# The opening of a hybrid encoder step: token tiles turned in threes, two projections chunk by chunk

## What is computed

```python
def rmsnorm(x, g):
    xf = x.astype(jnp.float32)
    y = xf * lax.rsqrt(jnp.mean(xf * xf, axis=-1, keepdims=True) + EPS) * g.astype(jnp.float32)
    return y.astype(x.dtype)

def even_layer(x, ...):
    h = rmsnorm(x, g_pre)
    proj = jnp.einsum('bld,de->ble', h, w_in)
    u, v, za, zb, xbc, dt_raw = jnp.split(proj, EVEN_SPLITS, axis=-1)
    ya, v_rows = gmlp_branch(u, v, za, ws, bs, gv)
    yb, s_fin, new_ctx = ssd_branch(zb, xbc, dt_raw, ...)
    ...

def ssd_branch(zb, xbc, dt_raw, ...):
    xbc, new_ctx = causal_dwconv(xbc, conv_ctx, conv_w, conv_b)
    xbc = jax.nn.silu(xbc)
    ...
    dt = jax.nn.softplus(dt_raw + dt_bias)
    a = -jnp.exp(a_log)
    # in the recurrence: acs = cumsum(dt * a), exp(acs) and so on
```

## Time and profile before

| what | value |
|---|---|
| median of three runs | 1696.01 us |
| the profiled execution | 1696.7 us, span 1694.9 us |
| TensorE busy | 1587.4 us (94%), matmuls 9562 |
| VectorE busy | 809.8 us (48%) |
| ScalarE busy | 669.2 us (39%) |
| GpSimd busy | 440.1 us (26%) |
| mean granted clock of TensorE | 0.976 |

### The profile page before, as it was taken

The page is one execution under the profiler, slowest core; times in us unless marked ns, Lnnn a source line. Parts: engine busy times, 40 slices in busy tenths (PEclk is TensorE's granted clock), DMA queues, the critical chain, the costliest instruction groups (busy, mean ns, idle before and its releaser), DMA issues.

```text
span 1694.9 us, 26649 instructions
## 1 busy us (share of the span) xinstructions
PE 1587.4 (94%) x9562; PEld 1462.9 (86%) x9562; DVE 809.8 (48%) x1753; ACT 669.2 (39%) x1243; POOL 440.1 (26%) x267
## 2 busy tenths in 40 slices
PE   5899999998999999999997999999999999995798
PEld 5899999998998999888886998889889898884576
DVE  5755677664883321336565543443434433342332
ACT  6433333332233332335454344545445445542221
POOL 1113453343212121244442212221213122232000
PEclk9999999999999999999998999999999999997899
DMA  4121213112102111154554444723323342222122
GB/s 143 39 65 56 67 56 97 55 43 67 50 13 66 38 49 37 58 178 150 172 190 88 77 60 42 70 40 63 56 41 70 43 69 41 68 68 75 38 82 75
DMA packets 128740, 121.06 MB, mean 71 GB/s; under 512 B 9706, under 2 KB 112500, under 8 KB 128684
## 3 DMA queue, kind: packets, MB, share of 16 engines
q1 hardware_dynamic: 128684, 120.30, 29.1%
HBM read 101.61 MB, written 18.66 MB: 71 GB/s over the span
## 4 chain that ended last, share of the span: by engine, by line
PE 79%; issue 6%; DVE 6%; ACT 5%; POOL 1%; DMA 1%; SPq 0%; POOLq 0%; ACTq 0%; DVEq 0%
PE PB L720 74%; PE PB L724 5%; DVE NRML L1737 2%; POOL WOL L698 1%; ACT L1239 1%; ACT L1629 1%; ACT SB L1701 1%; ACT WH L1233 0%; DMA XS<-in_x_prompt_dram 0%; ACT NRMH L1233 0%; DMA nf_rows<-NFROW 0%; ACT PT L1233 0%; DVE DTROW L1737 0%; POOL WL L604 0%; DVE XT L1744 0%
## 5 line engine op out<-in xcount | busy, mean ns | idle before, releaser
L720 PE MATMUL PB<-HH,WH 128*128 128x352 f32 x1872 | 620.9, 332 | 14.6 <-ACT XR L1253 6.0
L720 PE MATMUL PB<-HH,WL 128*128 128x352 f32 x1872 | 605.0, 323 | 0.0
L720 PE MATMUL PB<-HL,WH 128*128 128x352 f32 x1872 | 604.4, 323 | 0.0
L720 PEld LDWEIGHTS PB<-HH,WH 128*128 128x128 f32 x1872 | 355.2, 190 | 28.7 <-issue 20.4
L720 PEld LDWEIGHTS PB<-HL,WH 128*128 128x128 f32 x1872 | 355.8, 190 | 0.0
L720 PEld LDWEIGHTS PB<-HH,WL 128*128 128x128 f32 x1872 | 354.5, 189 | 0.0
L604 POOL TENSOR_TENSOR WL<-WRAW,WH 128x1024 fp32r<-128x1024 f32 x82 | 200.5, 2446 | 565.3 <-ACT WH L1233 550.0
L1233 ACT ACTIVATE WH<-WRAW 128x1024 fp32r<-128x1024 f32 x112 | 117.7, 1052 | 26.6 <-DMA WRAW<-in_w_in_even_dram 19.3
L1737 DVE TENSOR_TENSOR Y<-PB,Y 128x128 f32 (+2 forms) x72 | 20.2, 281 | 163.8 <-PE PB L720 163.8
L1701 ACT ACTIVATE SB<-SB,small 128x128 f32<-128x128 f32 (+8 forms) x72 | 53.8, 748 | 81.3 <-DVE small L1741 81.3
L720 PE MATMUL PB<-PT,VTOK 128*128 128x128 f32 (+2 forms) x624 | 82.2, 275 | 0.0
(11 more groups left out here) (290 smaller groups left out, 2453.0 us busy)
## 6 DMA issues: line engine op xcount, KB each, us to landing
WRAW<-in_w_out_even_dram SPq DMA_DIRECT2D x48, 512.0 KB, 3.5
WRAW<-in_w_in_even_dram SPq DMA_DIRECT2D x44, 512.0 KB, 3.8
WRAW<-in_w_in_odd_dram SPq DMA_DIRECT2D x32, 512.0 KB, 8.3
ACSB<-acs_rows SPq DMA_DIRECT2D x16, 528.0 KB, 4.8
NFB<-nf_rows SPq DMA_DIRECT2D x8, 656.0 KB, 3.9
XS<-in_x_prompt_dram SPq DMA_DIRECT2D x8, 512.0 KB, 6.0
XT<-in_x_prompt_dram SPq DMA_DIRECT2D x8, 512.0 KB, 4.8
x_rows<-OG SPq DMA_DIRECT2D x8, 512.0 KB, 5.3
```

The lines of the kernel that those rows point to most:

```text
L720: return pe.matmul(out, lhsT, rhs, start=start, stop=stop)
```

## The change

Tokens are taken in three groups of three tiles (`TRIPLES`), and PSUM banks 3, 4 and 5 serve in turn (`RING`). ScalarE's and VectorE's orders are written out: after three tiles are normalised, their turned blocks are read, with the squares, roots and norms of the later tiles in between. The time-step weights are split before the first reads, the first B weights between the first and the second group. TensorE takes chunk 0 of the time-step and of B tile 0, then chunk 1 of both, then chunk 2 of both, with the later groups' turns between the steps; B tile 0 uses banks 7, 6 and 5. Each step waits for its own low part. ScalarE's reads of the two tiles wait for the alternate counts of `p_chunk`. On SP's queue the time-step weights move ahead of x tile 3, the parameter rows behind it, and the first B weights between x tiles 5 and 6. VectorE's means, norms and low parts follow the same written order, and its `DEXP` copy stands behind the third norm. The diff, cut where it repeats the old or only names a helper:

```diff
+TRIPLES = [(0, 3 * P), (3 * P, 3 * P), (6 * P, 2 * P + DEC)]
+RING = (3, 4, 5)
...
@@ -358,6 +360,8 @@
         for b in range(NB):
             sp.dma_start(XS[:, b, :], xp[:, b, :]).then_inc(S(f"x_in{b}"), 16)
             if b == 2:
+                load_w(tile_no(W_DT, 1, 0), even(DT0, HEADS_B), HEADS_B)
+            if b == 3:
                 for src, (row, n) in (
                         (norm_pre[0].rearrange("(k p) -> k p", p=P), (PRE0, 8)),
                         (ssd_norm_g[0].rearrange("(k p) -> k p", p=P), (GSSD, 8)),
@@ -366,14 +370,14 @@
                         (state_conv[0, 0].rearrange("r (k p) -> (r k) p", p=P), (CTX, 36))):
                     sp.dma_start(ROWS[row:row + n, :], src).then_inc(S("rows_in"), 16)
                 sp.dma_start(DSM[:, :], ssd_d[0].rearrange("(t j) -> t j", j=2)).then_inc(S("rows_in"), 16)
-            if b == 3:
-                load_w(tile_no(W_DT, 1, 0), even(DT0, HEADS_B), HEADS_B)
+            if b == 5:
+                load_w(tile_no(W_BC, 1, 0), even(XBC0 + 8 * P))
         sp.dma_start(XS[0:DEC, NB, :], x_sample[0]).then_inc(S(f"x_in{NB}"), 16)
         sp.dma_start(CONVW_SB[:, :, :], conv_w[0].rearrange("(t p) k -> p t k", p=P)).then_inc(S("par_in"), 16)
         sp.dma_start(DTB[0:HEADS_B, :], dt_bias[0].unsqueeze(1)).then_inc(S("par_in"), 16)
         sp.dma_start(AL[0:HEADS_B, :], a_log[0].unsqueeze(1)).then_inc(S("par_in"), 16)
         sp.dma_start(BF[0:HEADS_C, :], b_forget[0].unsqueeze(1)).then_inc(S("par_in"), 16)
-        for j in range(4):
+        for j in range(1, 4):
             load_w(tile_no(W_BC, 1, j), even(XBC0 + (8 + j) * P))
 
 
...
-        first = tile_no(0, 1, 0)
-        for q, (b0, nb, rows) in enumerate(QUADS):
-            pe.wait_ge(S("xn"), b0 + nb)
-            for k in range(KT):
-                i = q * KT + k
-                if i >= 4:
-                    pe.wait_ge(S("h_lo"), i - 3)
-                for j in range(nb):
-                    last = turn(PB[3 + i % 4][:, j * P:j * P + rows], XS[0:rows, b0 + j, k * P:(k + 1) * P])
-                last.then_inc(S("x_t"), 1)
-                if q == 1:
-
-                    project_chunk(first, first, 0, HH, HL, ks=[k])
-        pe.wait_ge(S("h_lo"), 24)
-        for c in (1, 2):
-            project_chunk(first, first, c, HH, HL)
-        for w in range(1, W_XZ):
+
+        def x_turn(g, k):
+
+            i = g * KT + k
+            if k == 0:
+                pe.wait_ge(S("xn"), 3 * g + 3)
+            if i >= len(RING):
+                pe.wait_ge(S("h_lo"), i - len(RING) + 1)
+            for j in range(3):
+                b = 3 * g + j
+                rows = sample_rows(b)
+                last = turn(PB[RING[i % 3]][:, j * P:j * P + rows], XS[0:rows, b, k * P:(k + 1) * P])
+            last.then_inc(S("x_t"), 1)
+
+        def first_step(w, c, bank, k):
+
+            if k == 0:
+                pe.wait_ge(S("w_low"), w + 1)
+            pe.wait_ge(S("h_lo"), c * KT + k + 1)
+            cols = slice(c * CH, (c + 1) * CH)
+            mm(PB[bank][:, 0:CH], WH[:, w, k, :], HH[:, k, cols], start=k == 0, stop=False)
+            mm(PB[bank][:, 0:CH], WH[:, w, k, :], HL[:, k, cols], start=False, stop=False)
+            last = mm(PB[bank][:, 0:CH], WL[:, w, k, :], HH[:, k, cols], start=False, stop=k == KT - 1)
+            if k == KT - 1:
+                last.then_inc(S("p_chunk"), 1)
+
+        for k in range(KT):
+            x_turn(0, k)
+        for k in range(KT):
+            if k >= 4:
+                x_turn(1, k - 4)
+            first_step(W_DT, 0, 0, k)
+        for k in range(KT):
+            if k < 4:
+                x_turn(1, k + 4)
+            first_step(W_BC, 0, 7, k)
+        for k in range(KT):
+            if k >= 4:
+                x_turn(2, k - 4)
+            first_step(W_DT, 1, 1, k)
+        for k in range(KT):
+            if k < 4:
+                x_turn(2, k + 4)
+            first_step(W_BC, 1, 6, k)
+        for k in range(KT):
+            first_step(W_DT, 2, 2, k)
+        for k in range(KT):
+            first_step(W_BC, 2, 5, k)
+        for w in range(W_BC + 1, W_XZ):
             project(tile_no(w, 1, 0), tile_no(w, 1, 0), HH, HL)
 
 
...
+        def x_square(b):
+            rows = sample_rows(b)
+            act.wait_ge(S(f"x_in{b}"), 16)
+            if b > 0:
+                act.wait_ge(S("x_ss"), b)
+            act.activation(SQJ[0:rows, :], XS[0:rows, b, :], ACT.Square, accum_out=SS[0:rows, b:b + 1]) \
+                .then_inc(S("x_ss"), 1)
+
+        def x_root(b):
             rows = sample_rows(b)
             act.wait_ge(S("x_ms"), b + 1)
             act.activation(RT[0:rows, b:b + 1], MS[0:rows, b:b + 1], ACT.Sqrt).then_inc(S("x_rt"), 1)
-            if b == 2:
-
-                act.wait_ge(S("rows_turn"), 1)
-                order(copy(COLS[:, :], PB[3][:, 0:N_ROWS]))
-                copy(DCOL[:, :], PB[3][:, P:P + 8]).then_inc(S("cols"), 1)
+
+        def x_high(g, ks):
+            for k in ks:
+                i = g * KT + k
+                c0, n = TRIPLES[g]
+                act.wait_ge(S("x_t"), i + 1)
+                act.activation(HH[:, k, c0:c0 + n], PB[RING[i % 3]][:, 0:n], ACT.Copy,
+                               scale=COLS[:, PRE0 + k:PRE0 + k + 1]).then_inc(S("h_hi"), 1)
+
+        x_square(0)
+        x_square(1)
+        x_root(0)
+        x_square(2)
+        x_root(1)
+        x_root(2)
+        act.wait_ge(S("rows_turn"), 1)
+        order(copy(COLS[:, :], PB[3][:, 0:N_ROWS]))
+        copy(DCOL[:, :], PB[3][:, P:P + 8]).then_inc(S("cols"), 1)
         order.fence()
         act.wait_ge(S("w_clear"), 1)
-        for w in range(2):
-            split_high(tile_no(w, 1, 0))
-        for q, (b0, nb, rows) in enumerate(QUADS):
-            for k in range(KT):
-                i = q * KT + k
-                act.wait_ge(S("x_t"), i + 1)
-                act.activation(HH[:, k, b0 * P:b0 * P + nb * rows], PB[3 + i % 4][:, 0:nb * rows], ACT.Copy,
-                               scale=COLS[:, PRE0 + k:PRE0 + k + 1]).then_inc(S("h_hi"), 1)
+        split_high(tile_no(W_DT, 1, 0))
+        x_square(3)
+        x_high(0, range(0, 4))
+        x_square(4)
+        x_root(3)
+        x_high(0, range(4, 8))
+        x_square(5)
+        x_root(4)
+        x_root(5)
+        split_high(tile_no(W_BC, 1, 0))
+        x_square(6)
+        x_high(1, range(0, 4))
+        x_square(7)
+        x_root(6)
+        x_high(1, range(4, 8))
+        x_square(NB)
+        x_root(7)
+        x_root(NB)
+        x_high(2, range(0, 8))
 
...
-        read_chunks(tile_no(W_DT, 1, 0), whole(RW[4], HEADS_B), rows=HEADS_B)
-        split_high(tile_no(W_DT + 2, 1, 0))
+        for c in range(3):
+            act.wait_ge(S("p_chunk"), 2 * c + 1)
+            copy(RW[4][:, c * CH:(c + 1) * CH], PB[c][0:HEADS_B, 0:CH]).then_inc(S(f"c_read{c}"), 1)
+        act.wait_ge(S("w_raw0"), loads_of_slot(tile_no(W_DT + 2, 1, 0)))
+        act.wait_ge(S("p_chunk"), 5)
+        copy(WH[:, 0, :, :], WRAW[:, 0, :, :]).then_inc(S("w_high"), 1)
         load_ln_exp()
         log1p_exp_steps(RW[5][:, :], RW[6][:, :], RW[1][:, :], RW[2][:, :], "dtc")
         act.wait_ge(S("par_in"), 64)
@@ -1319,7 +1381,13 @@
             w = tile_no(W_BC, 1, j)
             if j > 0:
                 act.wait_ge(S("conv"), j)
-            read_chunks(w, parted(XR, 3, SAMP))
+                read_chunks(w, parted(XR, 3, SAMP))
+            else:
+                for c in range(3):
+                    act.wait_ge(S("p_chunk"), 2 * c + 2)
+                    for cols, out in parted(XR, 3, SAMP)[c]:
+                        last = copy(out, PB[(7, 6, 5)[c]][:, cols])
+                    last.then_inc(S(f"c_read{c}"), 1)
             split_high(tile_no(W_BC + 2, 1, j))
             conv_silu(j, (BT, CT)[j // 2][:, j % 2, :])
             if j == 0:
...
+        def x_low(g, ks):
+            for k in ks:
+                i = g * KT + k
+                c0, n = TRIPLES[g]
+                cols = slice(c0, c0 + n)
                 dve.wait_ge(S("h_hi"), i + 1)
-                stt(HL[:, k, cols], PB[3 + i % 4][:, 0:nb * rows], COLS[:, PRE0 + k:PRE0 + k + 1],
+                stt(HL[:, k, cols], PB[RING[i % 3]][:, 0:n], COLS[:, PRE0 + k:PRE0 + k + 1],
                     HH[:, k, cols].bitcast(f32), ALU.mult, ALU.subtract).then_inc(S("h_lo"), 1)
+
+        x_mean(0)
+        x_mean(1)
+        x_norm(0)
+        x_mean(2)
+        x_norm(1)
+        x_norm(2)
+        dve.wait_ge(S("rows_in"), 112)
+        dve.tensor_copy(DEXP[:, :, :], DSM[:, :].unsqueeze(2).broadcast_to([8, 2, HP])).then_inc(S("dexp"), 1)
+        x_mean(3)
+        x_low(0, range(0, 4))
+        x_mean(4)
+        x_norm(3)
+        x_low(0, range(4, 8))
+        x_mean(5)
+        x_norm(4)
+        x_norm(5)
+        x_mean(6)
+        x_low(1, range(0, 4))
+        x_mean(7)
+        x_norm(6)
+        x_low(1, range(4, 8))
+        x_mean(NB)
+        x_norm(7)
+        x_norm(NB)
```

(43 more changed lines are left out.)

## The result

The changed kernel takes 1700.7 us (median of 12 runs, 1699.25 to 1702.48), the kernel before 1697.2 beside it (12 runs, 1694.89 to 1698.99): a ratio of 1.0021, 95% interval 1.0014 to 1.0029. It is 3.5 us slower. The forecast was 1697.3, 1.3 us slower than before, in a range of 1694.5 to 1701.0: the direction and the range hold, the size doesn't. The forecast also called it no change, within 0.2%; the measured 0.21% lies on that edge, with its interval on both sides.

A forecast was written before the change was run, and what follows sets the result against it. The prediction took the end of the third time-step chunk (45.94 us) to bound the kernel. Its later end, +1.3 us, plus 0 for the moved weight split, on a median of 1696.0 gave 1697.3 us, range 1694.5 to 1701.0.

The forecast's parts named there:

- What bounds it: Opening: it hands on the moment the third time-step chunk is done, 45.94 us before, not the B projections.
- The serial piece: VectorE and ScalarE work from the time-step's last matmul to B tile 2's start at 74.81: 28.9 us.
- Rival 1: TensorE's whole stream, through B tile 0's end, sets the end: -6.4 us, 1689.6; chance 6%.
- Start of the reads: ScalarE's first read of transposed tiles comes at 14.05 instead of 20.65, 6.6 us earlier.
- rival 3: Parameter rows land late, delaying the opening: 1698 to 1699.5; beyond 0.2% in 6%.
- The tiles of three: TensorE's opening in groups of three tiles: third time-step chunk done at 46.9 by schedule, taken as 47.3, +1.3 us.
- The steps at the lower level up to 23.7: First half of time-step chunk 0: 4 x 0.88 = 3.5 us, costing nothing because norm 5 ends at 24.1.
- 1.9 + 8 x 0.79 + 1.9: Time-step chunk 1 and B chunk 1 with the third group's turns on TensorE: 10.1 us, to 43.1.
- rival 2: TensorE's clock stays low in mixed turns and steps from 24 us on: +3.8 (1699.8) or +6.3 (1702.3); chance 12%.
- The 0.4 us taken for a late rise: Third time-step chunk's end taken at 47.3 rather than the scheduled 46.9, allowing for low-clock steps, worst 48.1.
- The moved weight split: B tile 2's split asks at 57.65 instead of 58.96: could save about 1.15 or cost up to 0.4; taken as 0.
- Behind B tile 0: TensorE stands about 6 us after B tile 0, ends B tile 1 near 68.5 to 70, ahead of B tile 2 at 76.

The follow-up runs named there:

- the swap: Changed kernel with B chunk 2 put ahead of time-step chunk 2 on TensorE: median 1703.0 us, ratio 1.0035 to the kernel before.
- the run with 128 rows: Changed kernel with the short token tile turned at 128 rows (zeros below row 32) instead of 32: 1698.9 us, ratio 1.0009 to the kernel before.
- time-step first: Changed kernel with all three time-step chunks ahead of all B chunks on TensorE: 1698.3 us, ratio 1.0007 to the kernel before.
- B chunk 1 last: Changed kernel with B chunk 1 alone put behind time-step chunk 2, short turns of 32 rows: 1696.9 us, ratio 0.9998 to the kernel before.
- more short turns: Changed kernel with one more 32-row turn behind each of the second group's eight turns: 1704.3 us, ratio 1.0046 to the kernel before.

## Why the prediction was right in direction and short in size

*What bounds it: right.* The forecast read from the earlier trace rows that the opening hands on one moment, the end of the third time-step chunk, and that B tile 0 done sooner only widens a hole. The serial piece came out at 28.89 us against 28.87, and all thirteen traces lie within 0.1 of each other. Rival 1 (TensorE's stream) falls by the swap.

*Start of the reads: right.* ScalarE's first read is at 14.17 in its timeline (14.27 in the chain), against 14.05. DSM released TensorE at 10.3, as the forecast took it from the earlier trace rows; rival 3 didn't occur.

*The tiles of three, up to 35 us: right.* Eighth turn 19.65 (19.55 to 20.2 forecast), second triple 23.85 (24.1), third group from 34.85 (34.9). The steps at the lower level up to 23.7 did not happen in this profile. In nine of the eleven profiles with this opening they did, and TensorE still waited for norm 5, as forecast; but the eighth turn, the last ahead of these steps, was slower with them (0.91 against 0.56 us), so that from it to the second group 4.55 us passed instead of 4.20. That is 0.35, not nothing.

*"1.9 + 8 x 0.79 + 1.9": the term that failed.* The 0.31 us for a turn "with the short tile" stands there without a row, just under the 0.33 of three turns of 128 rows. Nothing in the rows that the forecast used showed a 32-row turn beside 128-row work. Measured, turn and step take 1.075, and 8 x 0.285 = 2.3 us; 46.9 + 2.3 = 49.2 is the 49.34 found. That this is the short turn is shown from both sides: 2.1 us of it go when the tile has 128 rows, and eight more such turns add 8 x 0.36 = 2.9 elsewhere, 2.3 behind what a wait hides. The bound of that term was missing, since nothing in the sum was allowed above 0.31. The row that could have warned of it was in the trace: short loads with 0.23 us of idle ahead of them at 33.50. Everything behind the third group is late by about that much: chunk 2 49.34 for 47, B tile 0 53.1 for 51, the end of the hole 59.35 for 57, B tile 2 78.23 for 76.

*The range: held by luck.* Its upper end, 1701.0, was set by a low clock (rival 2), which did not come; the measured 1700.7 lies 0.3 inside it for a cause that no rival named, and chunk 2 at 49.34 just inside the 49.5 that the forecast gave as a sign of being wrong. The direction was no luck: without the 2.3 us the sum comes to 46.9 and the loss to some 1.2 us (an estimate, 3.5 - 2.3), and the run with 128 rows stays above the kernel before (1.0009).

*The clock, rival 2: did not occur.* The 0.4 us taken for a late rise weren't needed in this profile. TensorE's timeline in the opening, and that of the run with 128 rows (lines 729 and 725):

```profile
15.44 3.13 PE L728 MATMUL PB<-IDENT,XS 128*128 128x128 f32 x12 [1.00 <-DVE HL L1812]
19.65 0.55 PE L728 MATMUL PB<-IDENT,XS 128*128 128x128 f32 x3 [1.09 <-DVE HL L1812]
19.96 0.41 PE L724 MATMUL PB<-HH,WH 128*128 128x352 f32 x1
20.21 0.32 PE L724 MATMUL PB<-HL,WH 128*128 128x352 f32 x1
20.37 0.32 PE L724 MATMUL PB<-HH,WL 128*128 128x352 f32 x1
...
19.91 0.90 PE L729 MATMUL PB<-IDENT,XS 128*128 128x128 f32 x3 [1.08 <-DVE HL L1813]
20.90 0.49 PE L725 MATMUL PB<-HL,WH 128*128 128x352 f32 x1
21.20 0.49 PE L725 MATMUL PB<-HH,WL 128*128 128x352 f32 x1
```

Twelve transposes take 3.13 us, 0.26 each; the next three are 0.10 apart (19.65 to 19.96), and of the matmuls behind them the second starts 0.16 ahead of the third, the pace of the higher level. Only transposes had run before. So it is in two of the eleven profiles with this opening (this one and time-step first). In the nine others the same 24 transposes were followed by 8 to 12 matmuls 0.29 apart, the pace of the lower level, before it doubled, as the second half of the list shows; up to the third group that cost 0.35 to 0.67 us in the five that do the same work there. The rule that the forecast weighed from the Trainium skill ("TensorE: Matmul & The Clock Gate", Part 4: PE-mode transpose), that transposes don't bring the full clock, therefore doesn't hold without exception: this trace and the one before disagree with it, and the nine agree. What decides between them stays open. In one run, time-step first, the clock did fall in the third group after two waits; with 128 rows and the same waits it did not, in two profiles, though in those it had also risen later in the opening. That is no proof that the short turns did it: with short turns and no long wait (B chunk 1 last) it stayed up too, and the kernel before kept its low stretch with 128 rows. This stays open too.

*The moved weight split, taken at nothing: right.* It holds up VectorE as before, at another place: the copy at 61.44 takes 2.23 us instead of 0.17, and the first tap 1.33 instead of 3.34. From the copies to the last tap are 5.95 us, against 5.92. GpSimd's row answers to the earlier trace rows:

```profile
60.97 2.67 POOL L608 TENSOR_TENSOR WL<-WRAW,WH 128x1024 fp32r<-128x1024 f32 x1 [7.39 <-ACT WH L1269]
```

*Behind B tile 0: half right.* The hole of "about 6 us" is 6.2. But B tile 1 ends at 72.8 and not by 70. It starts 2.3 us later than forecast, and the clock had fallen in the hole: its 72 matmuls take 13.5 us, where 0.16 us each would be 11.5. A stretch of the changed kernel in that hole (columns as above):

```profile
56.00:59.00 3.00, 0.00 (x0) 0.00 (x0) 2.61 (x4) 2.39 (x4) 0.00 (x0) 0.57 0.24 73
```

It cost nothing, being followed by a second hole of 5.4 us. The rest of the profiles' 4.8 us of span (1.07 in the 144 matmuls from B tile 2 on, 25.65 against 24.58) is more than the medians show: that piece took 24.43 to 26.02 in the thirteen profiles, in no order that follows the edits.

## What to carry to other kernels

Ask which single moment a stage hands on, and count every instruction that is put ahead of it: work that fills no wait delays it in full, and work that ends sooner beside it is lost in the next hole. Price an instruction by a row of its own shape in the same company; fewer rows or columns need not be cheaper. A repair of one cost (the padding) is worth something only where that cost is on the path: 2.1 us of the third group in the changed kernel, nothing that could be measured in the one before. And one profile is one execution: here the clock alone moved the opening by up to 0.7 us from one to the next.

## What the hardware did that was not expected

- A transpose of 32 rows among work of 128 rows costs 0.36 to 0.38 us of TensorE (1.17 against 0.81 in the run with more short turns, 1.075 against 0.70 in the third group), where one of 128 rows costs 0.11 (0.33 for three). Its weight load starts 0.17 us after the one before it has ended, and the next 128-row load starts only behind it. The Trainium skill ("TensorE: Matmul & The Clock Gate", Part 2: LDWEIGHTS) says that a load of 32x128 takes as long as one of 128x128, since the columns count. The trace agrees that the load itself is no dearer (0.13 us, where one of 128 rows beside matmuls is 0.19); what the trace adds is that the 32-row one is not overlapped here, also where its matmul has 128 columns (148.56).
- A VectorE copy of three columns took 2.23 us (61.44 to 63.67) beside a GpSimd split of 128x1024 that ended at 63.64; it took 0.17 alone.
- Behind the same 24 transposes TensorE's pace had doubled before the first matmul in two of eleven profiles, and doubled only 8 to 12 matmuls later in nine.
- The same program came out 3.2 us below the kernel before on one chip and 1.7 on another (ratios 0.9984 and 0.9989, whose intervals overlap), so intervals of under 0.1% either way still left an order of two versions open.
